# Moving a head stage's SBUF buffers by 64 bytes, and making every projection in one run of 512 columns

## The reference, cut to what matters

```
hc = rmsnorm(ctx) * (1 + scale_c) + shift_c            # 256 context tokens
s_f, s_b = context_final_states(hc, w_in[:, :3072])    # values and two forget gates
hx = rmsnorm(x) * (1 + scale) + shift                  # 2048 tokens
p  = hx @ w_in                                         # 1024 -> 7168 columns
i_in, z_f, z_b, q_in, gate_a, u_f, gate_f = split_proj(p)
o  = scan forwards(q, k_f, v, s_f) + scan backwards(q, k_b, v, s_b)     # 8 heads of 128
out = concat(norm(o) * silu(gate_a), fourier(u_f) * silu(gate_f)) @ w_out
return rmsnorm(x + gate * out)
```

## The kernel before

| matmuls (moving, stationary) | distance before |
|---|---|
| values (front weights, tokens) | 64 |
| context's forget gates (`hc`, front weights), context's values (front weights, `hc`) | 0 |
| heads' projections (tokens, head weights) | 192 |
| tail, last product (`w_hi` at `base + 64` or `base + 80 KB + 128`; `f_hi` at `base + 64 KB + 64`, `a_hi` at `base + 168 KB + 128`), most of it | 0 |
| tail, Fourier tables (`tab_hi`, `p_hi`, both at `base +` so many KB `+ 128`) | 0 |

## Time and profile before

### The profile page before, as it was taken

One profiled execution on the slowest core, in us unless ns is written; L12 is line 12 of the kernel. 1 busy time (PEld: TensorE's weight loads), 2 busy tenths in 40 slices (PEclk: granted clock), 3 DMA queues, 4 the chain that ended last, 5 costly groups with the idle time before them and its releaser, 6 DMA issues.

```text
span 2164.6 us, 51147 instructions
## 1 busy us (share of the span) xinstructions
PE 2093.7 (97%) x21853; PEld 1811.9 (84%) x21853; DVE 1531.6 (71%) x3275; ACT 537.5 (25%) x964; POOL 74.9 (3%) x109
## 2 busy tenths in 40 slices
PE   5799999999999999999999999999997999999997
PEld 3799998789888888888888888898886887888886
DVE  4865854116787878778887878798998886565554
ACT  3721134111222222212212222222213443221121
POOL 0000101000000000000000000000000010000000
PEclk9999999999999999999999999999999999999998
DMA  8534555333333424243433334243335466435351
GB/s 305 179 122 144 178 163 155 113 113 115 114 108 103 127 92 142 94 126 99 121 108 115 107 105 124 91 138 122 100 112 197 168 251 232 162 130 181 131 184 55
DMA packets 229876, 299.08 MB, mean 138 GB/s; under 512 B 14934, under 2 KB 159990, under 8 KB 226322
## 3 DMA queue, kind: packets, MB, share of 16 engines
q1 hardware_dynamic: 145346, 178.38, 25.4%
q10 hardware_dynamic: 73952, 81.18, 11.1%
q0 software_dynamic: 10352, 36.25, 5.2%
HBM read 198.16 MB, written 97.59 MB: 137 GB/s over the span
## 4 chain that ended last, share of the span: by engine, by line
PE 88%; DVE 6%; DMA 2%; ACT 1%; issue 1%; SPq 1%; ACTq 0%; DVEq 0%
PE all_bank L61 22%; PE all_bank L63 21%; PE all_bank L62 21%; PE all_bank L71 9%; PE all_bank L1573 3%; PE all_bank L1359 2%; PE all_bank L1529 2%; PE all_bank L1516 2%; PE all_bank L1566 1%; DVE hidden_h_lo L492 1%; PE all_bank L1555 1%; PE all_bank L1358 1%; PE all_bank L1017 1%; PE all_bank L2702 1%; SPq L375 1%
## 5 line engine op out<-in xcount | busy, mean ns | idle before, releaser
L61 PE MATMUL all_bank<-hidden_h_hi,head_hi 128*128 128x512 f32 x953 | 389.0, 408 | 0.4
L63 PE MATMUL all_bank<-hidden_h_hi,head_lo 128*128 128x512 f32 x953 | 374.2, 393 | 0.0
L62 PE MATMUL all_bank<-hidden_h_lo,head_hi 128*128 128x512 f32 x953 | 373.3, 392 | 0.0
L1612 ACT ACTIVATE head_projected<-all_bank 128x512 f32<-128x512 f32 x148 | 88.6, 599 | 741.4 <-PE all_bank L63 581.1
L63 PEld LDWEIGHTS all_bank<-hidden_h_hi,head_lo 128*128 128x128 f32 x953 | 178.9, 188 | 40.2
L61 PEld LDWEIGHTS all_bank<-hidden_h_hi,head_hi 128*128 128x128 f32 x953 | 179.1, 188 | 37.7 <-DVE head_lo L1654 1.7
L62 PEld LDWEIGHTS all_bank<-hidden_h_lo,head_hi 128*128 128x128 f32 x953 | 179.5, 188 | 32.3 <-issue 0.4
L1710 DVE RECIPROCAL head_inverse<-head_gate 128x448 f32<-128x448 f32 x64 | 185.0, 2925 | 0.0
L61 PE MATMUL all_bank<-front_hi,hidden_h_hi 128*128 128x256 f32 x512 | 143.6, 281 | 0.0
L63 PE MATMUL all_bank<-front_hi,hidden_h_lo 128*128 128x256 f32 x512 | 142.5, 278 | 0.0
L62 PE MATMUL all_bank<-front_lo,hidden_h_hi 128*128 128x256 f32 x512 | 142.5, 278 | 0.0
(11 more groups left out here) (314 smaller groups left out, 4710.9 us busy)
## 6 DMA issues: line engine op xcount, KB each, us to landing
head_raw<-in_w_in POOLq DMA_DIRECT2D x37, 512.0 KB, 4.8
head_value<-value_rows SPq DMA_DIRECT2D x64, 256.0 KB, 4.7
head_query<-piece_query SPq DMA_DIRECT2D x64, 256.0 KB, 5.8
head_out<-head_o ACTq DMA_DIRECT2D x64, 256.0 KB, 2.6
tail_o<-head_out SPq DMA_DIRECT2D x32, 512.0 KB, 5.8
front_raw<-in_w_in SPq DMA_DIRECT2D x19, 512.0 KB, 5.1
front_stage<-in_x SPq DMA_DIRECT2D x16, 512.0 KB, 6.3
front_w_mod<-in_w_ada SPq DMA_DIRECT2D x8, 1024.0 KB, 13.6
```

The costliest lines, as they stand in the source:

```text
L61: nc.tensor.matmul(out, st_hi, mv_hi, start=start, stop=False)
L62: nc.tensor.matmul(out, st_hi, mv_lo, start=False, stop=False)
L63: return nc.tensor.matmul(out, st_lo, mv_hi, start=False, stop=stop)
L1612: nc.scalar.activation(projected[unit % 2][:], ps_proj[unit % 2][:], PIECES[name][1], scale=PIECES[name][2]).then_inc(proj_copied, 1)
```

## The change

Every buffer of the heads that was placed at `work +` a multiple of 1 KB is placed 64 bytes higher (`hi`, `lo`, `raw`, values, keys, queries, gates, states, `near`, `o`), except those at `RAW`. The masks and `one_minus_lb` behind them move by the same 64 bytes. `hc_hi`, `hc_lo` move 64 bytes lower. The table `BY_COLUMNS` goes, and all projections of the heads are `mm3`. One `near` buffer now overlaps the front's output buffer by 64 bytes, so POOL waits for the front's last stores before it clears them. VectorE's wait for that moves from step 0 to step 2 of the first head, where `near` is first used.

```diff
-    hc_base = work + 60 * KB
+    hc_base = work + 60 * KB - HALF_LINE
...
-    BY_COLUMNS = {(0, 0): 20, **{(h, 0): 22 for h in range(1, HEADS - 1)}, (HEADS - 2, 1): 10, (HEADS - 2, 2): 15,
-                  (HEADS - 1, 0): 22, (HEADS - 1, 1): 22, (HEADS - 1, 2): 10}
...
-    HC, VALUES, QUERY_W, RAW, GATE_W, OUT_ROWS, LITTLE = (work + i * KB for i in (60, 44, 28, 0, 8, 24, 76))
+    RAW = work
+    HC, VALUES, QUERY_W, GATE_W, OUT_ROWS, LITTLE = (work + HALF_LINE + i * KB for i in (60, 44, 28, 8, 24, 76))
...
         pool.wait_ge(handed.product, handed.all_fills)
         pool.wait_ge(handed.gate_out, N_BLOCKS * DMA)
+        for sem in handed.stored:
+            pool.wait_ge(sem, handed.all_stored)
         for d in range(2):
             pool.memset(near[d][:], 0.0).then_inc(score_cleared, 1)
...
-                operands = (ps_proj[unit % 2][:], hi[b][:, k, :], lo[b][:, k, :], h_hi[group][:, k, :], h_lo[group][:, k, :])
-                if k and slot and by_columns[h, g] > 0:
-                    by_columns[h, g] -= 1
-                    done = mm3_by_columns(nc, *operands, k == KT - 1)
-                else:
-                    done = mm3(nc, *operands, k == 0, k == KT - 1)
+                done = mm3(nc, ps_proj[unit % 2][:], hi[b][:, k, :], lo[b][:, k, :], h_hi[group][:, k, :], h_lo[group][:, k, :],
+                           k == 0, k == KT - 1)
...
             if n == 0:
+                v.wait_ge(handed.masks_in, DMA)
+            if n == NG // 2:
                 v.wait_ge(score_cleared, 2)
-                v.wait_ge(handed.masks_in, DMA)
...
-            masks = s.at("masks", [P, 2, MASKED, P], work + WORK, U8)
-            one_minus_lb = s.at("one_minus_lb", [P, 2, HEADS], work + WORK + 2 * MASKED * P)
+            masks = s.at("masks", [P, 2, MASKED, P], work + WORK + HALF_LINE, U8)
+            one_minus_lb = s.at("one_minus_lb", [P, 2, HEADS], work + WORK + HALF_LINE + 2 * MASKED * P)
```

More of the change, by code:

```diff
@@ L1479, in _ @@
     def _(pe):
-        by_columns = {(h, g): BY_COLUMNS.get((h, g), 0) for h in range(HEADS) for g in range(NG)}
         def project_half(h, g, slot):
```

## The result

The change makes the kernel slower: 2197.9 us (median of 4 runs, 2196.24 to 2198.59) against 2167.64, a ratio of 1.0139 with a 95% interval of 1.0127 to 1.0151. The forecast was 2156.3, within 2151 to 2163. The profiled execution has a span of 2194.5 us, 29.9 more than before.

The account below looks back on a forecast made before the run. The prediction took TensorE alone to set the pace in the heads, up to the last step, and in the context. Gains of 5.7 + 3.7 + 2.0 - 0.2 = 11.2 us took 2167.48 to 2156.3 us, range 2151 to 2163.

Parts of the forecast that it names:

- Heads' triples at 227.4 ns: Heads' 953 triples of 512 columns: pitch from 229.4 to 227.4 ns at distance 0, gaining 5.7 us.
- Rival D: Distance 0 is slow in the heads too, pitch 233.0 ns, so the kernel gets slower: 2175.9 us; chance 0.06.
- C: Rival: addresses don't matter, only removing the column halves gains, 2.4 us, giving 2165.1 us; chance 0.10.
- Context: Context's matmuls of 256 columns leave distance 0: from 120.0 ns to between 113.3 and 117.8, gaining 2.0 us.
- Column halves: Heads' 256-column halves at distance 192: pitch 117.8 or 113.3 ns, nothing between, mean 116.4 ns.
- VectorE as the next bound: Heads: VectorE's tightest delivery, 0.67 us early, holds; the wait at seven head starts grows, costing 0.2 us.
- Rival B: Heads 6 and 7 give nothing because VectorE sets the pace there: 2158.6 us; chance 0.13.
- A: The forecast itself, all gains kept: 2156.3 us, own range 2152 to 2158.5; chance 0.71.
- POOL's new wait: First head: clears wait for the front's last stores, second piece's rounding up to 0.8 us later, costed at nothing.
- The 231 triples by columns: Heads: six halves at 116.4 ns become three matmuls at 227.4, 16.2 ns a triple, gaining 3.7 us.

Follow-up runs that it names:

- experiment 8: Changed kernel with idle instructions filling each step to 1,024, none near the beginning of a projection run; 2154.53 us against 2166.89 for the kernel before, ratio 0.9938.
- experiment 10: Kernel before with only the context's tokens placed 64 bytes lower; 2162.29 us against 2166.89, ratio 0.9985.
- experiment 1: Changed kernel with the table of column halves put back for 231 triples; 2164.34 us against 2165.88 for the kernel before, ratio 0.9987.

## Why the prediction was wrong

- *Heads' triples at 227.4 ns*: right. A run after, its first and last start, and the window with 35 matmuls: 7.73 us for 34 pitches, 227.4 ns (229.4 in the earlier trace rows). Over all runs of nine or more such matmuls at full clock, from the fourth on, the mean is 229.4 before and 227.7 in experiment 8, so the step is nearer 1.7 than 2.0 ns. Rival D, 233 ns, is out, and so is C.

```profile
528.27 0.39 PE L62 MATMUL all_bank<-hidden_h_lo,head_hi 128*128 128x512 f32 x1
...
536.00 0.40 PE L63 MATMUL all_bank<-hidden_h_hi,head_lo 128*128 128x512 f32 x1
...
528.50:536.10 7.60, 7.60 (x35) 1.00 0.11 39
```

- *Context*: the pitch was right. One run takes 5.34 us for 47 pitches, 113.6 ns, in place of 120.0. The means, in which the beginnings of the runs count too, went from 121.0 to 115.9 for the forget gates and from 120.7 to 118.7 for the values, which makes 2.3 us (2.0 forecast); experiment 10, where only these addresses differ, has the same means as the changed kernel. The kernel gained somewhat more: in ten profiled executions with the new place the first burst began at 512.0 to 515.6 us, and at 516.5 to 518.0 with the old in three, 3.4 us apart by the means. What the other 1.1 us are is open.

```profile
228.76 0.29 PE L61 MATMUL all_bank<-front_hc_hi,front_hi 128*128 128x256 f32 x1
...
234.10 0.28 PE L63 MATMUL all_bank<-front_hc_hi,front_lo 128*128 128x256 f32 x1
...
229.00:234.05 5.05, 5.05 (x47) 1.00 0.76 216
```

- *Column halves*: the mean of 116.4 ns stands, but 20 of the chain's 47 runs are listed there with 121.7 to 126.2 ns a half, since their time holds the entering of the run. "Nothing lies between" is true only with that taken off.
- *VectorE as the next bound*: right, 0.2 us at each head's start as before, 1.9 us in all against 1.7. Rival B is out: with padding that costs nothing (experiment 8) heads 6 and 7 take 5.3 us less than before, part of it small stops that the kernel before has there, and more than A gave them.
- *POOL's new wait*: nothing, as costed. The clears begin at 512.62, behind the stores, and no TensorE wait follows; experiment 1 holds them all.

```profile
512.62 0.98 POOL L1406 MEMSET head_near<- 128x512 f32 x2 [49.20 <-DMA value_rows<-front_out]
```

- *The 231 triples by columns*: the step that failed. The working was 6 x 116.4 ns against 3 x 227.4, and it holds as far as it goes (at the new distance the halves cost 0.8 us in a step with 22, experiment 1 against 8). But it priced matmuls by their pitch alone, and took the removal of 1,386 instructions out of 44,385 as nothing besides, without a reason. Their number was what kept the block boundaries out of the bursts. Against experiment 8, which has the same matmuls, the changed kernel loses 33.0 us in heads 0 to 5 and 8.7 in heads 6 and 7 (919.8 - 886.8, 225.5 - 216.8), and 4.5 in the last step and behind. No rival had this; the slower one, D, was another mechanism.

The forecast gain was there in size: experiment 8 measured 2154.5, where 2156.3 was forecast. That it is so near is partly luck. By the profiles the front gave 4.7 us where 2.0 was forecast, heads 0 to 5 gave 5.7 where 130 x 16.2 ns + 830 x 6.0 ns = 7.1 was, and heads 6 and 7 up to step (7,2) gave 5.3 where 2.4 was, in part from small stops that the forecast knew nothing of.

It could have been read. The kernel before has, beside the row, this one in its waits, which the prediction passed over. Its longest stop is in the last step:

```profile
PEld all_bank L1516 <- issue: 13.3, 23, 3.8
```

A stop of 3.8 us with "issue" behind it, in a run of small matmuls for which everything is ready, is what an instruction fetch looks like; 693 matmuls, 173 packets and table entries that make a head 4,097 instructions long were there to be put beside it.

The Trainium skill has the mechanism, in the page "Runtime: NRT & Kernel Launch", section "Instruction fetch mechanics": instructions come in 16 KiB blocks of 256, the next page is fetched while the current one runs, and crossing a boundary is "mostly hidden". This case's trace agrees with the size (16.4 KB, 256 instructions) and, for projections, with the hiding. It does not for bursts of small matmuls: all 57 boundaries at places 310 to 384 stopped TensorE for 1.6 to 3.8 us.

Open are the smaller stops in heads 6 and 7, which come in some executions and not in others at equal places, and the exact moment at which a block is ordered. What fills the 1.2 to 1.5 us between a packet's end and the block's first instruction is open too.

## What to carry to other kernels

Adding or removing instructions on an engine moves everything behind them against the blocks in which its instructions are fetched. Where a kernel alternates between long matmuls and bursts of tiny ones that are more than about 300 instructions long (150 matmuls with their loads), count the instructions from burst to burst, look for stops of 2 to 4 us with no releaser inside a burst, and see whether their places differ by multiples of 256. A change in instruction count should be compared at equal phase: pad the shorter version, or try it at a few offsets, before its time is believed. Here padding cost nothing only from the third triple of a run of projections on (from the second in heads 6 and 7).

## What was not expected of the hardware

- Six of the eleven stops of 1.8 to 3.5 us were followed by a stretch at a low granted clock (0.58 over 4 us in step (0, 3)), in which 512-column matmuls start every 0.42 us in place of 0.23. In heads 0 to 5 TensorE stood still for 21.4 us more than in experiment 8, and they took 33.0 us more.
- One instruction of two waits for a value long reached takes 106 ns from its start to the next one's; 132 ahead of the first triples cost 1.2 us a step, 49 further into the runs cost nothing that can be seen.
- 49 NOPs in a lump were hidden behind full-width matmuls; 97 were not: step (6,1) took 5.9 us more than in experiment 8.
- The pitch changed when an operand moved by 64 bytes: 256 columns 120.0 ns at distance 0 and 113.3 or 117.8 at 64 and 192; 512 columns the other way, 227.4 at distance 0 and 229.4 at 192. Every version here shows its distance's values. That the distance counts modulo 256 bytes is how I wrote it down; no run tests it.
